# Rows of seven experts stored in DRAM and fetched by row number, with changes to the mixer, the front and the router, in a two-layer hybrid block on one Trainium2 core

## What is computed

```python
for l in range(DEPTH):                       # 2 layers
    h = rmsnorm(x, attn_norm_g[l])
    x = x + hybrid_mixer(h, ...)             # moba + GLA + mLSTM
    # layer 0: swiglu with D_FF = 2816; layer 1:
    logits = (xt @ router_w) + router_b
    top_logit, top_e = lax.top_k(logits, 2)
    gate = softmax(top_logit)
    # for each expert e: y = (silu(x_e @ w_gate[e]) * (x_e @ w_up[e])) @ w_down[e]
    # out[token] += gate * y   for both picks of every token
```

## Time and profile before

| | us |
|---|---|
| median of 3 runs | 1545.37 (1543.23 to 1545.9) |
| profiled execution, its own time | 1545.86 |
| its span, first to last instruction | 1544.1 |
| PE busy | 1516.3 (98%) |
| DVE busy | 1231.9 (80%) |
| ACT busy | 946.0 (61%) |
| POOL busy | 37.9 (2%) |
| DMA | 412.71 MB, mean 267 GB/s |

### The profile page before, as it was taken

How to read it: one execution, slowest core, us unless ns; L and a number is a source line. 1 busy time by engine, 2 the same in 40 slices (tenths; PEclk the granted TensorE clock), 3 DMA queues, 4 the chain that set the end, 5 groups by cost and what they waited for, 6 DMA issues and landing times.

```text
span 1544.1 us, 19326 instructions
## 1 busy us (share of the span) xinstructions
PE 1516.3 (98%) x7534; PEld 1267.2 (82%) x7534; DVE 1231.9 (80%) x1218; ACT 946.0 (61%) x881; POOL 37.9 (2%) x69
## 2 busy tenths in 40 slices
PE   8999999999999999999899999999999999999996
PEld 6898888888888898888678888888888888888885
DVE  5778876655547688866699998989989999899996
ACT  6347534544435356534677777777777777777775
POOL 2000000000000000001000000000000000000000
PEclk9999999999999999999999999999999999999998
DMA  8544545455554455546799998999989999999980
GB/s 297 212 166 141 191 175 191 174 189 191 191 191 166 177 184 183 180 164 242 308 367 377 348 372 327 360 376 347 372 321 372 370 353 355 341 363 370 351 305 29
DMA packets 114802, 412.71 MB, mean 267 GB/s; under 512 B 13264, under 2 KB 13568, under 8 KB 114704
## 3 DMA queue, kind: packets, MB, share of 16 engines
q1 hardware_dynamic: 111872, 402.52, 69.7%
q0 software_dynamic: 2688, 8.61, 1.7%
q10 hardware_dynamic: 144, 0.26, 0.0%
HBM read 410.29 MB, written 1.05 MB: 266 GB/s over the span
## 4 chain that ended last, share of the span: by engine, by line
PE 91%; DVE 5%; ACT 2%; issue 1%; DMA 1%; SPq 0%; DVEq 0%; ACTq 0%
PE ps L1100 31%; PE ps L665 19%; PE ps L1111 14%; PE ps L966 8%; PE ps L655 4%; PE ps L943 4%; PE ps L644 3%; DVE w_lo L1665 2%; PE ps L1054 1%; DMA raw_m<-dense_dram 1%; PE ps L1078 1%; DVE w_lo L1521 1%; PE ps L1063 1%; ACT w_hi L1179 1%; PE ps L623 0%
## 5 line engine op out<-in xcount | busy, mean ns | idle before, releaser
L1665 DVE TENSOR_TENSOR w_lo<-late,w_hi 128x2048 fp32r<-128x2048 f32 x192 | 438.1, 2290 | 38.7 <-ACT w_hi L1241 38.6
L1241 ACT CAST w_hi<-late 128x2048 fp32r<-128x2048 f32 x192 | 367.3, 1913 | 44.3 <-PE ps L1100 44.3
L1521 DVE TENSOR_TENSOR w_lo<-raw_m,w_hi 128x2048 fp32r<-128x2048 f32 x115 | 262.6, 2290 | 130.7 <-ACT w_hi L1179 130.4
L1179 ACT CAST w_hi<-raw_m 128x2048 fp32r<-128x2048 f32 x115 | 218.2, 1906 | 132.7 <-PE ps L665 54.7
L1100 PE MATMUL ps<-w_hi,hT_hi 128*128 128x512 f32 x704 | 281.9, 400 | 2.3 <-DVE w_lo L1665 2.3
L1100 PE MATMUL ps<-w_hi,hT_lo 128*128 128x512 f32 x704 | 274.9, 390 | 0.0
L1100 PE MATMUL ps<-w_lo,hT_hi 128*128 128x512 f32 x704 | 274.6, 390 | 0.0
L665 PE MATMUL ps<-w_hi,hT_hi 128*128 128x512 f32 x464 | 183.6, 396 | 3.5 <-DVE w_lo L1521 3.5
L1665 DVE TENSOR_TENSOR w_lo<-raw_m,w_hi 128x2048 fp32r<-128x2048 f32 x72 | 165.4, 2298 | 24.2 <-ACT w_hi L1241 24.2
L665 PE MATMUL ps<-w_hi,hT_lo 128*128 128x512 f32 x464 | 181.0, 390 | 0.0
L665 PE MATMUL ps<-w_lo,hT_hi 128*128 128x512 f32 x464 | 180.7, 389 | 0.0
(11 more groups left out here) (343 smaller groups left out, 2158.2 us busy)
## 6 DMA issues: line engine op xcount, KB each, us to landing
late<-experts_dram SPq DMA_DIRECT2D x384, 512.0 KB, 4.7
raw_m<-dense_dram SPq DMA_DIRECT2D x233, 512.0 KB, 4.0
raw_m<-experts_dram SPq DMA_DIRECT2D x144, 512.0 KB, 4.4
bias<-b_in_dram POOLq DMA_DIRECT2D x26, 256.0 KB, 4.8
xt<-x_dram SPq DMA_DIRECT2D x4, 256.0 KB, 8.2
tmp<-front_dram SPq DMA_DIRECT2D x3, 256.0 KB, 6.3
out_dram<-xn SPq DMA_DIRECT2D x3, 256.0 KB, 4.2
tmp<-w_small_dram POOLq DMA_DIRECT2D x2, 320.0 KB, 5.1
```

The source lines that it names most:

```text
L1179: copy(w_hi[:, g % RS, :], slot_raw(g, False)).then_inc(hi_ready, 1)
L1241: copy(w_hi[:, m % RS, :], slot_raw(m, True)).then_inc(hi_ready, 1)
L1521: tt(w_lo[:, g % RS, :], slot_raw(g, False), w_hi[:, g % RS, :], ALU.subtract)\
L1665: tt(w_lo[:, m % RS, :], slot_raw(m, True), w_hi[:, m % RS, :], ALU.subtract).then_inc(lo_ready, 1)
```

## The change

In short, part by part:

1. **Experts 0 to 6 of pass 0** (`by_rows`): no selection transposes, no scatter, no scaling by the gate. ScalarE copies the accumulators to yrow, GpSimd stores its 128 rows into y_rows in DRAM, and zeroes one extra row. In expert 1 VectorE computes for each token and pick the row number (`rows_of_picks`) and the gate (`gates_of_picks`, moved here from expert 0). In expert 7, GpSimd fetches 128 rows for each of two token tiles and two picks by indirect DMA into prow, one after the other, and VectorE adds them with their gate to xt at `dn` 5 to 8. Expert 7 keeps the scatter.
2. **late_split** holds only for the first gate group of experts 1 to 7.
3. **Router banks**: logits in bank 2, ranks in bank 4 (0 before); ten warming matmuls ahead of the claim of the logits' bank in place of five behind it.
4. **Moba**: probabilities are scaled on VectorE before their transposes, the product with the values gives the transposed result directly (`prob_values`), its split into yT_hi and yT_lo follows at once, and y_transposes(l, 0) and moba_rows go. The last head of group 1 is transposed one chunk later. The second half of the convolution taps and its Silu move behind g0'.
5. **Front**: chunk 3 gets memory of its own (mqk_flat) and is loaded ahead of cols and x; the last three column pieces are issued by ScalarE; GpSimd's first loads wait for chunk 3.
6. **End of the dense layer**: the last split on VectorE comes behind the loop.

The diff, cut to its core:

```diff
-                ("pT1", (6, 7, 4, 5)), ("lo", (2, 3)), ("pv1", (4, 5)), ("g0", (0, 1)), ("lc", (6,)),
-                ("gs", (4, 5, 7, 6)), ("yT0", (4, 5)), ("g0'", (2, 3)), ("go", (4, 5)), ("mb", (6, 7)),
+                ("pT1", (6, 7, 5, 4)), ("lo", (2, 3)), ("pv1", (5,)), ("g0", (0, 1)), ("lc", (6,)),
+                ("gs", (4, 5, 7, 6)), ("g0'", (2, 3)), ("go", (4, 5)), ("mb", (6, 7)),
-    fills(1, "logits", (0,))
+    fills(1, "logits", (2,))
-    fills(1, "rank", (0,))
+    fills(1, "rank", (4,))
+    def by_rows(pas, e):
+        return pas == 0 and e + 1 < E
...
+        yrow = nc.alloc_sbuf_tensor_at("yrow", [P, D], f32, offset=masks_at)
+        prow = nc.alloc_sbuf_tensor_at("prow", [P, D], f32, offset=masks_at + 4 * D)
+        y_rows = nc.dram_tensor("y_rows", ((E - 1) * P + 1, D), f32).ap()
...
         def slot_raw(n, moe):
+            if n == RM and not moe:
+                return mqk_flat
...
-                sp.dma_start(front[:, c], front_d[:, c]).then_inc(xT_in[i], 16)
+                if i < 2:
+                    c = slice(KT + k0 * T if k0 else 0, KT + k1 * T)
+                    sp.dma_start(front[:, c], front_d[:, c]).then_inc(xT_in[i], 16)
...
-                    if g >= RM:
+                    if g > RM:
                         sp.wait_ge(lo_ready, g - RM + 1)
                     load(g)
-                    if g == 2:
+                    if g == RM:
...
-            pool.wait_ge(piece_in[-1], 16)
+            pool.wait_ge(raw_in[0], 32)
...
+            for e in range(E - 1):
+                for h in range(2):
+                    b, k = FILL[(0, e), "acc", h]
+                    pool.wait_ge(drained[b], k + 1)
+                pool.dma_start(y_rows[e * P:(e + 1) * P, :], yrow[:, :]).then_inc(y_out, 16)
+            pool.wait_ge(zero_in, 16)
+            pool.wait_ge(y_out, 16 * (E - 1))
+            pool.wait_ge(picks_ready, 1)
+            for j in range(2 * NT):
+                if j:
+                    pool.wait_ge(rows_added, j)
+                pool.indirect_dma_start(out=prow[:, :], out_offset=None, in_=y_rows,
+                                        in_offset=bass.IndirectOffsetOnAxis(ap=row_u[:, j:j + 1], axis=0))\
+                    .then_inc(rows_in, 16)
...
             def prob_values(l, g):
                 for hh in range(4):
                     await_drained(l, f"pT{g}", hh)
+                b = claim(l, f"pv{g}")
                 for hh in range(4):
+                    p0, c0, v = HD * (hh % 2), hh // 2 * T, slice((4 * g + hh) * HD, (4 * g + hh + 1) * HD)
+                    mm(ps[p0:p0 + HD, b, c0:c0 + T], vm[:, 0, v], pT[:, hh, 0:T], start=True, stop=False,
+                       skip_group_check=True)
+                    ins = mm(ps[p0:p0 + HD, b, c0 + P:c0 + T], vm[:, 1, v], pT[:, hh, T:T + P], start=False, stop=True,
+                             skip_group_check=True)
+                done(ins, l, f"pv{g}")
...
+            keep_warm(10)
             lg_bank = claim(1, "logits")
-            keep_warm(5)
...
-                    if (kind, i) == ("dn", NF - 1):
+                    if (kind, i) == ("dn", NF - 1) and by_rows(pas, e):
+                        if e:
+                            act.wait_ge(y_out, 16 * e)
+                        for h in range(2):
+                            b = await_full(l, "acc", h)
+                            copy(yrow[:, h * W:(h + 1) * W], ps[:, b, :]).then_inc(drained[b], 1)
...
+                link(V.reciprocal(sums[:, g, :, :], sums[:, g, :, :]))
+                tt(sc[:, g, :, 0:T], sc[:, g, :, 0:T], sums[:, g, 1, :].unsqueeze(2).to_broadcast([P, 4, T]), ALU.mult)
+                tt(sc[:, g, :, T:T + P], sc[:, g, :, T:T + P], sums[:, g, 0, :].unsqueeze(2).to_broadcast([P, 4, P]),
+                   ALU.mult).then_inc(p_scaled, 1)
...
-                conv_taps(l, 1)
-                ahead(l, "lo")
                 biased(l, "lo", lambda t: lo[:, t, :])
-                moba_rows(l, 1)
+                lo_of(l, "pv1", 0, yT_hi[:, 2:4, :], yT_lo[:, 2:4, :])
...
-                for i in range(2):
-                    lo_of(l, "yT0", i, yT_hi, yT_lo)
                 ahead(l, "g0'")
                 biased(l, "g0'", lambda t: gates[:, 1, t, :])
+                conv_taps(l, 1)
                 dve.wait_ge(gstat, 3 * l + 2)
...
-                            split_to(min(2 * NU + n + 2, LAYER_BASE[1]))
+                            split_to(min(2 * NU + n + 2, LAYER_BASE[1] - 1))
...
+            def rows_of_picks():
+                none = float((E - 1) * P)
+                link(tt(prod, oh, pos[:, :, 0:E].unsqueeze(1).to_broadcast([P, 2, NT, E]), ALU.mult))
+                link(V.reduce_sum(place.rearrange("p t a -> p a t"), prod, AX))
+                note(stt(row_f, idf[:, :, 0:2], float(P), place, ALU.mult, ALU.add))
+                link(ts(valid, idf[:, :, 0:2], E - 1.5, None, ALU.is_lt))
+                link(stt(valid, place, float(P), valid, ALU.is_le, ALU.mult))
+                link(stt(row_f, row_f, -1.0 - none, valid, ALU.add, ALU.mult))
+                ts(row_u.rearrange("p (t a) -> p t a", t=NT), row_f, none, None, ALU.add).then_inc(picks_ready, 1)
+
+            def add_picked(j):
+                dve.wait_ge(rows_in, 16 * (j + 1))
+                if j:
+                    dve.wait_ge(rows_added, j)
+                r = xt[:, j // 2, :]
+                stt(r, prow[:, :], row_gate[:, j:j + 1], r, ALU.mult, ALU.add).then_inc(rows_added, 1)
...
-                    late_split = kind == "gu" and c == 1 and i < 2
+                    late_split = e > 0 and (kind, i, c) == ("gu", 0, 1)
...
-                    if (e, kind, i) == (0, "dn", 2):
+                    if pas == 0 and (e, kind) == (1, "dn") and i in (3, 6):
+                        (rows_of_picks if i == 3 else gates_of_picks)()
+                    if pas == 0 and (e, kind) == (E - 1, "dn") and i in (5, 6, 7, 8):
+                        add_picked(i - 5)
```

More of the change, by code:

```diff
@@ L318, in program @@
         rbias = bflat[:, 1480:1488]
+        prod = bflat[:, 1152:1184].rearrange("p (a t n) -> p a t n", a=2, t=NT)
+        place = bflat[:, 1496:1500].rearrange("p (t a) -> p t a", t=NT)
+        valid = bflat[:, 1500:1504].rearrange("p (t a) -> p t a", t=NT)
+        row_f = bflat[:, 1504:1508].rearrange("p (t a) -> p t a", t=NT)
+        row_u = bflat[:, 1508:1512].bitcast(u32)
+        row_gate = bflat[:, 1512:1516]
         g12 = bflat[:, 1488:1496].rearrange("p (t n) -> p t n", t=NT)
@@ L702, in scores, with prob_transposes @@
                     done(mm(ps[:, b, T:T + P], q[:, 0:P], k[:, 0:P], start=True, stop=True), l, f"s{g}", hh)
-            def prob_transposes(l, g):
-                pe.wait_ge(p_ready, 2 * l + g + 1)
-                for hh in range(4):
+            def prob_transposes(l, g, heads):
+                pe.wait_ge(p_scaled, 2 * l + g + 1)
+                for hh in heads:
                     b = claim(l, f"pT{g}", hh)
                     for j in range(3):
-                        ins = nc.tensor.transpose(ps[:, b, j * P:(j + 1) * P], sc[:, g, hh, j * P:(j + 1) * P],
-                                                  ident[:, :])
+                        o = (j + 1) % 3 * P
+                        ins = nc.tensor.transpose(ps[:, b, o:o + P], sc[:, g, hh, j * P:(j + 1) * P], ident[:, :])
                     done(ins, l, f"pT{g}", hh)
@@ L847, in _ @@
                 unit(l, "lk")
-                prob_transposes(l, 0)
+                prob_transposes(l, 0, range(4))
                 unit(l, "lv")
                 prob_values(l, 0)
-                prob_transposes(l, 1)
-                unit(l, "lo")
+                prob_transposes(l, 1, range(3))
+                chunk(l, "lo", 0)
+                prob_transposes(l, 1, (3,))
+                chunk(l, "lo", 1)
                 prob_values(l, 1)
@@ L879, in _ @@
                     done(ins, l, "mb", i)
-                for i in range(2):
-                    await_drained(l, "yT0", i)
+                for g in range(2):
+                    await_drained(l, f"pv{g}")
                 unit(l, "up0")
@@ L1244, in _ @@
             A(y0, ident[:, 0:2], ACT.Copy)
+            for i in range(2, len(PIECES)):
+                c = slice(KT + PIECES[i][0] * T, KT + PIECES[i][1] * T)
+                act.dma_start(front[:, c], front_d[:, c]).then_inc(xT_in[i], 16)
             for k in range(KT):
@@ L1286, in _ @@
                 A(sc[:, 0, :, :], sc[:, 0, :, :], ACT.Exp, scale=HD ** -0.5).then_inc(p_ready, 1)
-                ahead(l, "gr")
+                ahead(l, "lq", 0)
                 act.wait_ge(sub_ready, 2 * l + 2)
@@ L1324, in _ @@
                 A(gr, gr, ACT.Silu).then_inc(gate_ready, 1)
-                for u in range(2):
-                    act.wait_ge(conv3, 2 * l + u + 1)
-                    A(mqk[:, 4 * u:4 * u + 4, :], mqk[:, 4 * u:4 * u + 4, :], ACT.Silu).then_inc(mqk_ready, 1)
+                conv_silu(l, 0)
                 for i in range(2):
```

(3 more changed lines are left out.)

99 lines of the change are left out of this document (47 added, 52 removed).

## The result

The changed kernel takes 1519.72 us (median, 1518.56 to 1520.26), the kernel before 1545.05 beside it: ratio 0.9837, 95% interval 0.982 to 0.9854, so 25.3 us less where 24.1 were forecast. On record was 1521 in a range of 1515 to 1531. The profiled execution of the changed kernel took 1518.56 us with a span of 1516.6; its span is 27.5 us shorter than that of before. These two single executions lie a little further apart than the medians.

What follows compares the result with a forecast made beforehand. TensorE was taken as the bound nearly everywhere, with little VectorE cover. Terms 13.0 + 1.8 - 0.3 + 5.1 + 3.5 + 1.0 + 0 = 24.1 us; 1545.86 - 24.1 - 0.49 = 1521.3, say 1521, range 1515 to 1531.

Steps and rivals of the forecast that it cites:

- the rival's 6: VectorE becomes the bound where taps, picks and adds moved to it: upper ends +6 and +4, 1528 us, chance 14%.
- Scatter and selection transposes: Experts 0 to 6: 14 scatter groups of 0.93 us go, 13.0 us, and 14 selection transposes go, 1.8 us.
- Stalls of expert 0: Expert 0: the old gates stall goes, 1.3 us, and two stalls of 0.7 us where the split stood behind the product.
- Row numbers and gates in expert 1: New VectorE work for the picks: TensorE loses 0.65 us to the row numbers and 1.2 to the gates.
- Fetches: Last expert's four chained indirect fetches: from 4 to 12 us, taken as 6, hidden between adds 8.4 us apart.
- Slower: Rival, 4%: indirect fetch is slow, costing three times whatever exceeds 8.4 us; decides from 16.4 us a fetch.
- The router: Router: new banks remove the wait ahead of expert 0's gather and the clock fall; 5.1 us gained, about 2 if clock falls.
- The 20% rival: Router gain lost: the clock falls all the same or ScalarE's copies pace the gather; 3 to 4 us back, 1525.
- the products with the probabilities stay even: Mixer layers: products of probabilities and values take 2.7 us a group before, 2.6 after, so no gain.
- a stall of 0.9 us at the y_gla transposes: Mixer layers: moved taps make y_gla late, TensorE waits about 0.9 us a layer, a swap for 0.87 of transposes.
- The front: Start of kernel: fourth chunk's free memory and place ahead of x give 2.8 us, earlier request 0.7; 3.5, between 1 and 5.
- The rival of more relief: Corrections and additions gone from the experts' ends also remove seven stalls of 0.7 us: 1516 us, chance 8%.

Runs made afterwards that it cites:

- the kernel with four further edits: Changed kernel plus weight split ahead in experts 1 to 7, small column copy before its split, two fetch buffers, column table before chunk 3: 1510.9 us, ratio 0.9783.

## Why the prediction was right, and where it was not

**The bound.** TensorE as bound nearly everywhere held: work taken from it came back nearly whole. That the sum came within 1.2 us of the medians is in part luck: about 4 us were missing for the mixer and 1 for the gates and row numbers, while the front, the stalls of expert 0, the adds and the dense end were together some 3 us too high. VectorE did not become the bound: gates and adds cost about 2.5 us, not the rival's 6.

**Scatter and selection transposes.** 13.0 + 1.8 was right. By the traces an expert whose stretch has no other edit (4 to 6) gains 2.12 to 2.26 us; 2.11 was forecast (1.86 + 0.26). The estimate of 0.13 us for each transpose, nearer to the overlapped end, is of the right size: 0.30 us come back at each place where two stood. From one pair's gather to the next it is now 190.4 and 190.0 us; 190.2 was forecast.

**Stalls of expert 0.** 2.7 us forecast, 2.1 measured: 1.04 for the gates and 0.52 for each of the two splits. The prediction took 0.7 for a split, 0.3 for the longer chunk and 0.4 of idle time ahead of it. The chunk is 0.28 longer there too (3.01 in the changed kernel's chain above, 2.74 in that of the kernel with the split ahead), so that 0.24 are left for the idle time.

**Row numbers and gates in expert 1.** 0.65 and 1.2 forecast. Around the row numbers TensorE has no gap over 0.35 us; the gates cost about 0.7, a start-to-start gap of 0.92 at 905.83 where 0.23 is the rule.

**Fetches.** Assumed 6 us (4 to 12), hidden. The trace, POOL's timeline (the instruction itself, without the transfer) and the view of that line, last row (from issue to landing):

```profile
1417.12 1.50 POOL L620 DMA_INDIRECT prow<-y_rows,bias  x1 [5.78 <-issue]
1467.20 2.78 POOL L620 DMA_INDIRECT prow<-y_rows,bias  x1 [48.58 <-DVE xt L2056]
1475.66 4.95 POOL L620 DMA_INDIRECT prow<-y_rows,bias  x1 [5.68 <-DVE xt L2056]
1485.36 2.75 POOL L620 DMA_INDIRECT prow<-y_rows,bias  x1 [4.74 <-DVE xt L2056]
```

```profile
DMA to landing us min/median/max: 6.1/7.2/9.4
```

The value was too low and the bounds were right, but the first and third landed later than the 8 us that were to be the sign, and one fetch in four was not hidden. The third is issued at 1475.66 and lands 8.12 us later by the chain; add three then waits:

```profile
1483.81 1.28 DVE L2056 SCALAR_TENSOR_TENSOR xt<-prow,bias,xt 128x1024 f32<-128x1024 f32 x1 [0.96 <-DMA prow<-y_rows,bias]
```

Around this add TensorE falls back by 1.2 us, where the others cost 0.6 together: 1.8 against 1.2 in expert 7, and the miss is this one wait. It is there in five of the eight executions profiled with one buffer. In the kernels with the experts' part alone and with the taps back no add waits, and expert 7 loses 0.7 us, less than forecast; with the stores repeated it is the second add that waits, 0.84 us. The kernel with two buffers has no such wait. The prediction took 8.4 us, the distance between two adds, as the limit of a fetch. But the fetch waits for the add before it, so the distance of 8.46 us loses 1.27 for that add and 0.27 until the issue, and 6.9 are left; 8.12 is 1.2 over it. The break-even of the rival *Slower* was put 1.5 us too far out in the same way.

**The router.** 5.1 forecast, 5.2 in the profiled pair, 4.7 and 5.2 by the medians of the two kernels with this part, for the reason given: the shared bank. The kernel with two bank numbers changed alone shows it. The 20% rival fell. The sum was read from an execution of before with a long fall of the clock; against the three kernels of the last section the router's gain would be 4.0 to 4.4.

**The mixer: the step that failed** is "the products with the probabilities stay even ... 2.6 us" a group. The prediction counted columns for each head as if they ran one after the other. The turned products have 64 output partitions each, and neighbours in different halves run side by side: 1.5 us a group, which is 2.2 us a layer less. The head order shows it: 0.70 us for one head, 0.71 for two. The Trainium skill's page TensorEngine Tiling (Array Packing), Tiling Modes, says that tiles of 128x64 operate independently and that different tiles can execute matmuls in parallel; the trace agrees, and the diff's slice of output partitions by hh % 2 was there to be read with it. An estimate by that rule before the run would have been half of 2.6, 1.3 us a group.

The second part of that step, a stall of 0.9 us at the y_gla transposes, failed too. The statistic did come later against TensorE, by 2.4 us, nearly as forecast (14.5 us ahead of the transposes, 168.93 to 183.44, against 16.9, 171.04 to 187.91 in the timeline of before). But between the statistic and y_gla VectorE of before had idle time ahead of a split and for ScalarE, 1.1 us, which is gone now, and the whole way is 1.5 us shorter:

```profile
172.83 2.29 DVE L1521 TENSOR_TENSOR w_lo<-raw_m,w_hi 128x2048 fp32r<-128x2048 f32 x1 [0.37 <-ACT w_hi L1179]
175.87 0.17 DVE L1530 TENSOR_TENSOR st<-st 128x8 f32<-128x8 f32 x1 [0.75 <-ACT st L1345]
```

So y_gla came only 0.9 later against its transposes (1.7 us ahead of them here, 2.6 before), inside its margin. Summed: 0.87 for the transposes + 2.2 for the products - 0.8 or so for the new stall at the scores (taking it away gave 1.0 and 0.9) = 2.3 a layer, against 2.3 and 2.4 measured.

And the prediction looked at the taps only where they went. With the products shorter, VectorE's chain ahead of the GLA scores would have been the bound, and in the one execution that was run a wait of 2 us there brought the clock down too: the kernel with the taps at the old place loses 5 us a layer. Had the change left them there, its mixer would have come out some 6 us slower and not 4 faster.

**The front.** 3.5 forecast, 2.2 in the profiled pair, 2.5 with that part alone. The stall ahead of the fourth chunk (chunk 3) went, as said. A good part of the rest went to a wait that the prediction did not look for: the small column table now queues behind that chunk too, and VectorE's wait for the table stands ahead of its next split:

```profile
18.38 2.29 DVE L1570 TENSOR_TENSOR w_lo<-raw_m,w_hi 128x2048 fp32r<-128x2048 f32 x1 [1.68 <-DMA cols<-cols_dram]
```

The split does not read the table, so the wait could have been put behind it as well; no run tried that. Of a load that is moved in a queue, the ones that now stand behind it count too. In the kernel with the table loaded ahead of chunk 3 this wait is gone and the front is 0.7 us shorter, though the front differs by more than that between executions. The 0.7 us forecast for the early request do not show: with all pieces on one queue the medians are the same.

**The end of the dense layer.** 1.0 forecast, 0.6 net. The stall is gone and gives 1.0 at its place, but TensorE of the changed kernel comes there 0.4 us late, by a small wait ahead of the last transposes of hidden rows. The kernel with the mixer's part alone has that wait too, so it comes from there. This edit was not run alone.

**The rival of more relief** (8%, the seven stalls go) did not come: the split stood behind the product in one chunk per expert still, and the scatter that had covered the first such place was gone. The kernel with the split ahead shows what it would have given.

## What to carry to other kernels

Read the output partitions of small matmuls, not only their columns: two products of 64 output columns in different halves cost one, if they follow one another. Work moved off a queue is worth most where it leaves, so look at the source of a move with the other gains of the change already taken: each gain brings the next engine's chain closer. A transfer moved ahead in a queue is paid by the small ones behind it, and by whoever waits for them earlier than needed.

## What the runs showed of the hardware

**The fetch and VectorE.** The indirect DMA instruction takes POOL 1.03 us at its shortest (the first of the kernel with four further edits), and 2.75 to 4.96 where it starts within the first of two weight splits on VectorE. In the changed kernel the second began at 1467.20 and ended at 1469.98; VectorE's timeline there:

```profile
1466.85 4.49 DVE L1709 TENSOR_TENSOR w_lo<-raw_m,w_hi 128x2048 fp32r<-128x2048 f32 x2
...
1475.31 4.48 DVE L1709 TENSOR_TENSOR w_lo<-late,w_hi 128x2048 fp32r<-128x2048 f32 x2
```

By the mean of 2.24 for each of the two, the first ends at 1469.1 and the instruction 0.9 us after it. The third fetch (1475.66 to 1480.61) ends 0.8 us after the second split of its pair (1479.79). In the kernel with the taps back the third took 2.75 us. That fits an instruction that stands behind one split or behind two, while the splits beside it keep their 2.24 to 2.29 us. The Trainium skill's page SBUF, section on the two sides, has the port pair as an exclusive lock of whoever starts first, with the other blocked; the trace agrees: the split had started first (1466.85 against 1467.20), and the fetch is the one that waits. The prediction had laid that wait, 2 us, on the splits. What decides between one split and two was not settled.

**The clock after short waits.** TensorE idled 2.89 us in the router of before and 2.05 us in the kernel with the taps back, and both times the granted clock then read 0.50, for 6.7 us and for some 10 us. The length of the wait does not settle it: at the front TensorE idled 2.41 us ahead of the fourth chunk in before and 2.85 us ahead of the second piece in the changed kernel, and the clock read 1.00 over both. After the 0.50 us at the GLA scores of the changed kernel it stayed up, by the window over it:

```profile
150.00:155.00 5.00, 4.50 (x51) 3.79 (x47) 5.00 (x7) 1.47 (x3) 0.20 (x1) 1.00 0.58 225
```

With the taps back a wait of 2 us cost 5.6 in the end, 3.5 of them net by the clock.

**The DMA rate.** With the stores repeated the two-expert window carried 391 GB/s with a share of 0.99 and TensorE hardly waited; the highest rate seen in a slot-filling stretch of before was 408.

**The same code at two clocks.** The kernels with the experts', the mixer's and the front's part alone have the router of before. TensorE stood still there for the same 2.89 to 2.90 us, but the gather took 5.50 to 5.55 us, not 6.62, and expert 0 began 0.8 to 1.2 us earlier. The chain and a window of the one with the front's part:

```profile
743.59 2.89 issue
746.48 5.50 PE ps L1057 x32
```

```profile
746.00:750.00 4.00, 3.52 (x17) 3.55 (x18) 0.54 (x4) 1.75 (x3) 0.00 (x0) 0.57 1.04 410
750.00:756.00 6.00, 5.75 (x34) 4.92 (x33) 4.68 (x5) 3.08 (x4) 0.00 (x0) 1.00 0.39 156
```

The front differs in the same way. The middle of the fourth chunk started at 31.2 us in the profiled execution of before, and at 33.0 and 33.2 in the kernels with the experts' and the mixer's part alone, whose front is that of before. The windows of before and of the mixer's part alone:

```profile
28.00:33.00 5.00, 4.68 (x21) 3.87 (x22) 3.35 (x12) 4.97 (x7) 0.00 (x0) 1.00 0.63 236
```

```profile
28.00:33.00 5.00, 3.91 (x12) 3.13 (x13) 3.35 (x11) 4.97 (x8) 0.00 (x0) 0.75 0.65 250
```

The clock fell in one and not in the other. That is as much as some edits here are worth; for these the local rows and a median of several executions have to agree.
